# First layer's prompt attention: gate and sum folded into a diagonal factor, the causal mask added by a product

## The reference

```python
s = q @ k.T * (HEAD_DIM ** -0.5)
s = where(mask, s, NEG)                 # causal
p = exp(s - max(s)); l = sum(p)
o = (p / l) @ v                         # once for k_sel, v_sel, once for the window's
o_nsa = gate[0] * o_cmp + gate[1] * o_sel + gate[2] * o_win
```

## Time and profile before

| | before |
|---|---|
| median of 3 runs | 3657.1 us (3653.39 to 3663.52) |
| profiled execution, own time | 3654.23 us |
| its span | 3651.9 us |
| TensorE busy over the span | 3029.6 us (83%) |
| VectorE | 1379.9 us (38%) |
| ScalarE | 892.0 us (24%) |
| GpSimd | 992.3 us (27%) |

### The profile page before, as it was taken

How to read it: one execution, slowest core, us unless ns; L and a number is a source line. 1 busy time by engine, 2 the same in 40 slices (tenths; PEclk the granted TensorE clock), 3 DMA queues, 4 the chain that set the end, 5 groups by cost and what they waited for, 6 DMA issues and landing times. The chain is left out here.

```text
span 3651.9 us, 48433 instructions
## 1 busy us (share of the span) xinstructions
PE 3029.6 (83%) x20203; PEld 2740.1 (75%) x20203; DVE 1379.9 (38%) x2706; ACT 892.0 (24%) x1572; POOL 992.3 (27%) x457
## 2 busy tenths in 40 slices
PE   6665785977678899977978878889988788889998
PEld 6542675944468899977867767789966688879998
DVE  6663410078432422242644463321045211242224
ACT  4210220044112411132321231222122110342212
POOL 2220120034103533333322122233234000353331
PEclk9766897589669999988987788799988766999999
DMA  4102225341012222222200120013210320222221
GB/s 144 38 0 69 59 65 85 93 193 53 29 29 75 64 81 81 82 69 77 72 14 24 37 60 25 14 58 97 68 42 1 115 87 29 90 68 83 81 81 61
DMA packets 219654, 237.10 MB, mean 65 GB/s; under 512 B 40972, under 2 KB 186700, under 8 KB 218830
## 3 DMA queue, kind: packets, MB, share of 16 engines
q1 hardware_dynamic: 204734, 229.39, 20.4%
q10 hardware_dynamic: 14704, 4.63, 0.6%
HBM read 212.06 MB, written 48.35 MB: 71 GB/s over the span
## 5 line engine op out<-in xcount | busy, mean ns | idle before, releaser
L270 POOL TENSOR_TENSOR WRr<-WR,WH 128x2048 fp32r<-128x2048 f32 (+3 forms) x98 | 442.6, 4516 | 957.5 <-ACT WH L258 957.5
L2020 PE MATMUL PS<-HH,WRr 128*128 128x288 f32 x1152 | 343.1, 298 | 0.0
L410 PE MATMUL PS<-HH,WH 128*128 128x288 f32 (+1 forms) x928 | 278.7, 300 | 52.0 <-PEq L96 52.0
L410 PE MATMUL PS<-YTr,WRr 128*128 128x288 f32 x1024 | 304.6, 297 | 0.0
L410 PE MATMUL PS<-YTr,lt_WX 128*128 128x288 f32 x1408 | 281.8, 295 | 0.0
L410 PE MATMUL PS<-HTr,WH 128*128 128x288 f32 (+1 forms) x928 | 278.0, 300 | 0.0
L410 PE MATMUL PS<-HH,WRr 128*128 128x288 f32 (+1 forms) x928 | 278.0, 300 | 0.0
L258 ACT CAST WH<-WR 128x2048 fp32r<-128x2048 f32 (+3 forms) x98 | 180.4, 1842 | 386.9 <-DMA WR<-in_mlp_w 192.8
L2020 PE MATMUL PS<-HH,WH 128*128 128x288 f32 x768 | 228.6, 298 | 9.5 <-POOL HTr L2008 8.7
L410 PE MATMUL PS<-WH,HH 128*128 128x256 f32 (+3 forms) x760 | 219.6, 289 | 18.8 <-PEq L96 18.8
L410 PEld LDWEIGHTS PS<-YTr,lt_WX 128*128 128x128 f32 x1408 | 227.1, 188 | 0.1
(11 more groups left out here) (631 smaller groups left out, 6889.6 us busy)
## 6 DMA issues: line engine op xcount, KB each, us to landing
WR<-in_mlp_w SPq DMA_DIRECT2D x64, 1024.0 KB, 5.6
WR<-in_cd_w_in SPq DMA_DIRECT2D x34, 1024.0 KB, 5.4
out_dil_s<-in_cache_dil_kv SPq DMA_DIRECT2D x2, 7936.0 KB
WR<-in_ab_w_in SPq DMA_DIRECT2D x10, 1024.0 KB, 5.3
HT<-in_cache_dil_kv SPq DMA_DIRECT2D x16, 512.0 KB, 5.0
d_V<-in_cache_dil_kv SPq DMA_DIRECT2D x16, 512.0 KB, 5.0
past_rows<-in_cache_nsa_kv SPq DMA_DIRECT2D x16, 256.0 KB, 3.4
YT<-in_state_ssm ACTq DMA_DIRECT2D x16, 256.0 KB, 4.6
```

The costliest lines, as they stand in the source:

```text
L270: pool.tensor_tensor(K.WRr[:, n % RING, 0:used], K.WR[:, n % RING, 0:used], high_slot(K, i, used).bitcast(F32), ALU.subtract).then_inc(K.l ...
L410: last = pe.matmul(out, a, b, start=(n == 0), stop=(n == 3 * len(terms) - 1))
L2020: last = pe.matmul(out, a[:, k, c], h[:, k, x], start=(n == 0), stop=(n == 3 * KT - 1))
```

## The change

Three edits in `nsa_prompt`:

1. The mask is added on TensorE. After the two score products, which now leave their accumulation open, two more products add `ident.T @ CM`, so `CM`, to the diagonal block of each g. VectorE's addition is gone.
2. The gate and 1/sum are no longer multiplied into E. VectorE builds for each g a diagonal matrix `DR = ident * (1/sum) * gate` (128x128, two buffers, one instruction with two scalars per partition), and `turn` computes `E_tile.T @ DR` by a plain product where it had a transpose. The output is the transposed tile with its columns scaled.
3. GpSimd has no instruction in the stage. The semaphores `rg_ready`, `p_even` and `p_odd` become one, `d_ready`.

```diff
-                        last = pe.matmul(K.PS[:, 2 * (u % 2) + g, 0:(i + 1) * P], QT[r, m, i * P:(i + 1) * P],
-                                         KTT[r, j, 0:(i + 1) * P], start=True, stop=True)
+                        pe.matmul(K.PS[:, 2 * (u % 2) + g, 0:(i + 1) * P], QT[r, m, i * P:(i + 1) * P],
+                                  KTT[r, j, 0:(i + 1) * P], start=True, stop=False, skip_group_check=True)
+                    for g in range(2):
+                        last = pe.matmul(K.PS[:, 2 * (u % 2) + g, i * P:(i + 1) * P], K.ident[:], K.CM[:],
+                                         start=False, stop=True, skip_group_check=True)
                     last.then_inc(s_mm, 1)
...
-                    pe.wait_ge(p_even, u + 1)
-                    pe.wait_ge(p_odd, u + 1)
+                    pe.wait_ge(d_ready, u + 1)
...
-                            last = pe.transpose(K.PS[:, 4 + g, k * P:(k + 1) * P], E[:, u % 3, g, k * P:(k + 1) * P], K.ident[:])
+                            last = pe.matmul(K.PS[:, 4 + g, k * P:(k + 1) * P], E[:, u % 3, g, k * P:(k + 1) * P], DR[:, u % 2, g, :],
+                                             start=True, stop=True)
...
-            @block.gpsimd
-            def _(pool):
-                for u in range(N):
-                    L = (units[u][1] + 1) * P
-                    pool.wait_ge(rg_ready, u + 1)
-                    pool.tensor_scalar(E[:, u % 3, 0, 0:L], E[:, u % 3, 0, 0:L], sm[:, u % 3, 0:1], None,
-                                       ALU.mult).then_inc(p_even, 1)
...
-                    diag = K.PS[:, b:b + 2, i * P:L]
-                    do(dve.tensor_tensor(diag, diag, bc(K.CM[:], 1, 2), ALU.add))
...
-                    dve.tensor_tensor(sm[:, u % 3, :], sm[:, u % 3, :],
-                                      GT[:, i, :].rearrange("p (j g m) -> p j g m", j=3, g=2)[:, j + 1, :, m], ALU.mult).then_inc(rg_ready, 1)
-                    dve.wait_ge(rg_ready, u + 1)
-                    L = (i + 1) * P
-                    dve.tensor_scalar(E[:, u % 3, 1, 0:L], E[:, u % 3, 1, 0:L], sm[:, u % 3, 1:2], None, ALU.mult).then_inc(p_odd, 1)
+                    if u >= 2:
+                        dve.wait_ge(turned, u - 1)
+                    for g in range(2):
+                        at = (j + 1) * NH + g * REP + m
+                        last = dve.tensor_scalar(DR[:, u % 2, g, :], K.ident[:], sm[:, u % 3, g:g + 1], GT[:, i, at:at + 1],
+                                                 ALU.mult, ALU.mult)
+                    last.then_inc(d_ready, 1)
```

More of the change, by code:

```diff
@@ L1618, in nsa_prompt @@
         E = sb("p_E", [P, 3, 2, SEQ])
+        DR = sb("p_DR", [P, 2, 2, P])
         PT = K.HT[:].rearrange("p k n -> p (k n)")[:, 0:2048].rearrange("p (a b t n) -> p a b t n", a=2, b=2, t=NT)
@@ L1621, in nsa_prompt @@
         sm = sb("p_sm", [P, 3, 2])
-        with stage(nc, "s_mm", "nm_ready", "exp_done", "rg_ready", "p_even", "p_odd", "turned", "t_act", "t_dve", "pv_done",
-                   "y_out", "dve_link") as (block, s_mm, nm_ready, exp_done, rg_ready, p_even, p_odd, turned, t_act, t_dve,
+        with stage(nc, "s_mm", "nm_ready", "exp_done", "d_ready", "turned", "t_act", "t_dve", "pv_done",
+                   "y_out", "dve_link") as (block, s_mm, nm_ready, exp_done, d_ready, turned, t_act, t_dve,
                                             pv_done, y_out, dve_link):
@@ L1700, in _ @@
                         act.wait_ge(turned, u - 2)
-                        act.wait_ge(rg_ready, u - 2)
+                        act.wait_ge(d_ready, u - 2)
                     for g in range(2):
```

## The result

The changed kernel takes 3680.5 us (median, 3677.5 to 3682.9), the one before 3656.5; the ratio is 1.0059 with a 95% interval of 1.0043 to 1.0076. Forecast were 3684 in 3662 to 3698. The medians differ by 24 us, where +27 was forecast. The profiled execution took 3677.5 us, 23.3 more than before's own 3654.2.

What follows compares the result with a forecast made beforehand. A chain of waits between engines was taken to bound the stage, and TensorE after the change: floor 209 + stalls 8 + ends 7 = 224 us against 197, +27, so 3684 us, range 3662 to 3698.

Steps and rivals of the forecast that it cites:

- The floor: TensorE's work in `nsa_prompt`: 143 us plus 37 for the transposing product and 29 for the mask, 209 us.
- the price of 0.112 a record: Plain f32 products in the second layer took 0.112 us a record, so 0.224 a product against 0.11 a transpose.
- the fixed part of `turn`: Each group of transposes in `turn` costs 0.15 us once, besides 0.11 a record.
- The bound of +10 us: Between mask and `turn` a gap of 0 was taken; three waits at 0.15 us each time would add +10.
- The stalls: TensorE waits in `turn` for ScalarE's copy: 0.42, 0.13 and 0.43 us, 1.0 per eight units, 8 us in all.
- The ends: Start and end of the stage: 1 us first exponential, 2 last copies, 4 half-speed clock; 7 us.
- VectorE and GpSimd: In the stage VectorE loses some work, which buys nothing; GpSimd's 82 us go, having cost time only through the wait.
- A: Rival: array shape switches between TensorE groups cost nothing once TensorE is behind; stage 202 us, total 3662; chance 0.07.
- B: Rival: the diagonal product in `turn` is as cheap as a transpose; stage 197 us, no change; chance 0.08.
- C: Rival: the diagonal product in `turn` costs four transposes, 106 us in place of 37, total 3753; chance 0.02.
- e1's rival: For the mask's product alone: each product adds its full price to the stage, +29 us, 226 us.

Runs made afterwards that it cites:

- e4: Changed kernel with ScalarE's copy of unit u - 2 ahead of the exponentials of unit u, instead of u - 3's; stage 218.8 us against 223.4.
- e7: Changed kernel with the mask's product in fp32r, nothing else; stage 212.1 us against 223.4, one run 3669.1 us.
- e5: Kernel before with mask by f32 product, VectorE scaling both g, ScalarE making all copies ahead of the exponentials; stage 185.1 us against 196.8.
- e3: Changed kernel with the two mask products issued ahead of the score products, one more array shape change per step; stage 228.9 us against 223.4.
- e1: Kernel before with only the mask moved to TensorE products, gate and sum as before; stage 199.2 us against 196.8, ratio 1.0012.
- e9: Kernel before with ScalarE copying both g ahead of the exponentials, GpSimd still scaling g = 0; stage 195.2 us against 196.8.
- e10: Kernel before with VectorE scaling both g, copies where they were; stage 197.0 us against 196.8.
- e8: Kernel before with VectorE scaling both g and ScalarE copying both g ahead of the exponentials, mask on VectorE; stage 177.8 us, -0.51%.
- e6: As e5, but the mask's product takes fp32r copies of the identity and the mask; stage 174.2 us, ratio 0.9938 against the kernel before.

## Why the prediction was right

**The floor.** 26.1 us for eight units were forecast. In the timeline the scores' and the values' groups take what the earlier trace rows gave, the mask 0.44 (0.45 forecast), `turn` 1.99 (1.94). So the price of 0.112 a record, read from the second layer, held in this stage, and the fixed part of `turn` is 0.20 and not 0.15, 3 us over the stage.

**No gap between mask and `turn`.** Forecast 0, seen 0: from one load to the other it takes 0.44 (820.89 to 821.33), four records of 0.11. The bound of +10 us for it was not needed.

**The stalls.** Forecast were 0.42, 0.13 and 0.43 a group. The timeline has 0.47 (834.07 to 834.54), 0.03 and 0.42 (844.58 to 845.00). The places were right and the sum nearly so (0.92 for 1.0). The engine was wrong for the first, which ends with VectorE's copy behind that of y, a copy that I had left out of VectorE's queue. That its size came out all the same is luck: ScalarE's copy, by which it was reckoned, ends 0.09 us earlier. In e4, where ScalarE's copy comes sooner, this stall stays and the other two go.

**The ends.** 7 us were taken. A group takes 27.3 us in the timeline (27.1 forecast), so eight leave 4.8 of the 223.4. Of the 2 us less, the clock explains about one by my estimate: it rose 2 us sooner after the stage's start than in the kernel before, and two microseconds less at half speed are worth one. This offsets most of the 3 us of `turn`. So the stage's +26.6 for +27 is closer than its terms; both errors are small.

**VectorE and GpSimd.** Two things show that TensorE and not they bound the changed stage: VectorE waits 67.8 us for the mask's products, and in e7 0.22 us less of product per unit takes 11.3 us off it. e5, with GpSimd unused too, is 38 us shorter than the changed kernel, but it also moves the copies, so the 38 us are not the price of the diagonal alone.

**The rivals.** A is refuted by e3. B and C, another price for the diagonal's product, are refuted by the timeline (16 records in 1.99 us, where a transpose's price would give 1.03). That each edit adds its own price, as e1's rival had it, is refuted by e1.

Open is what in the switch makes the 0.20 us: e3 shows that the order of products of different shape costs it and a wait does not, not what the engine does meanwhile. Not run was the diagonal's product in fp32r, which in the mask's product halves the records.

## What to carry to other kernels

Work may be moved to an engine that waits, but only up to its slack: here TensorE had 54 us of it, the first edit's 29 us vanished in it, and the two together (66 us) overran it. Count the slack from groups that ran unheld, start to start, with what a change of the array's shape costs; the busy time alone (151 of 200 us) would have said 49. When a wait is the bottleneck, look for a second chain of the same length before cutting the first; e9 and e10 moved the stage by 1.6 us and 0.2 alone and by 19 together (e8). The fastest of the versions run is e6: mask by an fp32r product, scaling on VectorE, copies on ScalarE ahead of the exponentials, 0.62% below the kernel before.

## What the runs showed of the hardware

- At a granted clock of 1.00 a plain f32 product of 128 columns with a full array took 0.22 us from start to start (changed kernel, e1 to e5), an fp32r one 0.11 to 0.12 (e7, e6), a transpose of the same tile 0.11.
- A change between 64 and 128 rows of the array cost 0.20 us with no wait in between (e3, granted clock 1.00), and 0.25 to 0.27 at 0.50; the groups of this stage show 0.15 to 0.21 where the shape changes and a wait stands. A satisfied wait without a change of shape cost nothing visible (mask to `turn`).
- The granted clock was 0.50 when the stage began and rose some microseconds later, not always after the same time: about 8.6 us after the stage's first product in the changed kernel (0.50, 0.78 and 1.00 in the three stretches of five microseconds from 739; 0.78 puts the rise at 746.2) and 10.6 in the kernel before (0.50 up to 750). That TensorE was busy from the start in the one and waited in the other doesn't explain it: in e3 TensorE was busy from 740.3 on as well (8.66 of the 8.7 us up to 749), and the clock was still 0.50 up to 750, 9.7 us after that start. What sets the moment stays open.

```profile
...
749.00:750.00 1.00, 1.00 (x6) 0.47 (x3) 0.35 (x1) 0.00 (x0) 0.00 (x0) 0.50 1.18 508
750.00:751.00 1.00, 1.00 (x6) 0.65 (x7) 0.93 (x5) 0.42 (x2) 0.00 (x0) 0.76 0.00 0
```
